# Alternating the attention scores between the two halves of the partitions and two PSUM banks, masks gathered behind them

## The chip, the cores and the metric

One core of one Trainium2 chip runs the whole program as one launch. The metric is device time in microseconds (us), the median of a few runs. The core's engines work in parallel, each through its own instruction queue in order: TensorE (PE for matmuls, PEld for weight loads), VectorE (DVE), ScalarE (ACT), GpSimd (POOL) and SyncE (SP), which issues the loads of the weights. They wait for one another on semaphores.

## The reference, cut to what matters

Two transformer blocks of two layers each run on 256 tokens of width 1024 in float32. Attention comes five times in different forms: in both layers of the first block ("sel", each query keeps its 64 best keys), then in the second block MLA and dilated attention in layer 0, differential and MoBA attention in layer 1. With one batch and 256 tokens all of them come down to this, for query tile t of 128 tokens (tile 0 sees 128 keys, tile 1 sees 256):

```
s = q @ k.T                       # per head, depth 64 (96 in MLA)
s = s + mask                      # 0 or -1e30, a key that is not allowed
p = softmax(s * scale)            # row maximum, exp, sum
out = p @ v
```

Dilated attention has 12 heads in three groups (gp) with three mask patterns; the three scores of one output head h share one softmax.

## The kernel before, in words

The weights stream through three RAW slots of 128x2048 floats. ACT rounds each to WH, DVE makes the remainder WL, and a linear layer is three matmuls for each slice (lines 1355 to 1357). All order is written out by hand: the generators put parts in one list, `order`, and each engine's program walks that list and emits its own share of every part. So the list fixes the order on every engine, and only semaphores tie the engines to each other. PSUM has eight banks; `take()` takes the first of a queue of free banks with the events that free it, `give()` puts it back at the end.

An attention is a list of units. A unit is the work of a few heads of one query tile: four heads of 128 keys or two heads of 256 keys in sel, MLA and MoBA, two heads with two maps each in differential attention, one output head with its three groups in dilated attention. `attention()` runs them as a pipeline; its step k puts these parts in the list:

1. `scores` of unit k on PE (lines 1422 to 1436) and `soft` of unit k: DVE takes the row maximum of each PSUM bank (line 1856) and scales it (line 1866), ACT takes exp for each head out of PSUM into the buffer E (line 1460, the helper for every ACT instruction).
2. `turn` of unit k-1: PE transposes the exps (line 1380), ACT or DVE copies them to PET. Ahead of them stand `pad` matmuls on the identity (line 1340), whose results nobody reads; they fill waiting time.
3. Some steps of a filler: pieces of a linear layer, gating, or the transposes of the output.
4. `values` of unit k-2: PE multiplies with v (line 1447).

T holds q and k with depth on the partitions. Heads of depth 64 lie in pairs in one row of T: an even head on partitions 0 to 63, an odd head on 64 to 127. Before the change a unit of sel and MoBA has heads of one half alone (`par`) and one bank; a dilated unit has three heads of one half in two banks; a differential unit has its first map's heads in half 0 and one bank, its second map's in half 1 and another. In every unit each head's score matmul (line 1432) is followed by its mask matmuls (line 1434: the identity in bfloat16 as weights, the mask as moving data, adding into the same bank). A dilated head of tile 1 has two masks of 128 columns. A float32 matmul shows as two records in the trace, a bfloat16 one as one.

`sel_score` (line 1401) is other work with the same operands: the index scores of the key selection, two heads of half 0 into one bank, then two of half 1 into another, first for 128 keys and then for 256, with no mask between them.

Of the kernel before, what the change touches and what calls it, by code (L numbers as in the profile page):

```python
# [29 lines left out]
B_ID, B_TRI, B_UP, B_TRI4, B_M4, B_TRI16, B_M16 = range(7)  # L30
# [13 lines left out]
def plan():  # L44
# [130 lines left out]
def program(nc, W, xd, xTd, pTd, posd, pos2d, colvd, cstd, cstbd, vecd, sgwd, smalld, out):  # L175
    with ExitStack() as ctx:
# [65 lines left out]
        def maskb(b):  # L242
            return cstb[:, b * 128:b * 128 + 128]
# [409 lines left out]
        for i in range(2):  # L653
# [36 lines left out]
            tw = []  # L690
# [33 lines left out]
            for t in range(2):  # L724
                nk = 128 * (t + 1)
                ok = {}
                ok.update(normalised(ok, MIX[:, t, 0:512].rearrange("p (h d) -> p h d", h=8), SM[t], 8, 64))
                keys_.append(ok)
                per = 4 // (t + 1)
                for par in range(2):  # L730
                    hs = [par + 2 * j for j in range(4)]
                    for a in range(0, 4, per):
                        hh = hs[a:a + per]
                        segs = [(T[64 * par:64 * par + 64, h // 2, tok(t)], T[64 * par:64 * par + 64, 4 + h // 4, 0:nk],
                                 nk, [(0, nk, selb[:, t, 0:nk])]) for h in hh]
                        outs = [(h * 64, 64, [(n_ * (t + 1) + kb, H[:, kb, 640 + (h // 4) * 64:704 + (h // 4) * 64])
                                              for kb in range(t + 1)]) for n_, h in enumerate(hh)]
                        units.append(dict(banks=[segs], joint=False, diff=False, after=tw + [("sel", (i, t))],
                                          vafter=hw[0] + hw[1], sums=[SM[t][:, h:h + 1] for h in hh], outs=outs, ok=ok,
                                          blocks=[c * 128 for c in range(per * (t + 1))]))  # L740
# [180 lines left out]
        for i in range(2):  # L921
# [9 lines left out]
            if i == 0:  # L931
# [73 lines left out]
                for t in range(2):  # L1005
# [5 lines left out]
                    for a in range(0, 8, per):  # L1011
                        hh = list(range(a, a + per))
                        segs = [(T[0:96, h, tok(t)], T[0:96, 8 + h, 0:nk], nk, [(nk - 128, 128, maskb(B_TRI))])
# [3 lines left out]
                        units.append(dict(banks=[segs], joint=False, diff=False, after=tw, vafter=mvw, ok=ok,  # L1017
# [4 lines left out]
                t_pe = [keys_[1]["op"]]  # L1022
                tw2 = []
                for t in range(2):
                    for x0, base in ((0, 0), (768, 6)):
                        tw2 += turn_T([H[:, t, x0 + h * 128:x0 + h * 128 + 128] for h in range(6)], qkr[t] + t_pe,
# [4 lines left out]
            else:  # L1031
# [46 lines left out]
                for t in range(2):  # L1078
# [4 lines left out]
                    for a in (0, 2):  # L1083
                        bks = []
                        for mp in range(2):
                            bks.append([(T[64 * mp:64 * mp + 64, h, tok(t)], T[64 * mp:64 * mp + 64, 4 + h, 0:nk], nk,
                                         [(nk - 128, 128, maskb(B_TRI))]) for h in (a, a + 1)])
# [3 lines left out]
                        units.append(dict(banks=bks, joint=False, diff=True, after=tw, vafter=dw[2][0] + dw[2][1],  # L1091
# [20 lines left out]
            for t in range(2):  # L1112
# [5 lines left out]
                if i == 0:  # L1118
                    for h in range(4):
                        segs = []  # L1120
                        for gp in range(3):
                            hd = gp * 4 + h
                            bs = 64 * (hd % 2)
                            mk = [(nk - 128, 128, maskb((B_TRI, B_TRI4, B_TRI16)[gp]))]
                            if t:
                                mk.append((0, 128, maskb((B_UP, B_M4, B_M16)[gp])))
                            segs.append((T[bs:bs + 64, hd // 2, tok(t)], T[bs:bs + 64, 6 + hd // 2, 0:nk], nk, mk))
                        outs = [(h * 64, 64, [(gp * (t + 1) + kb, H[:, kb, 1536 + (gp * 4 + h) * 64:1600 + (gp * 4 + h) * 64])
                                              for gp in range(3) for kb in range(t + 1)])]
                        units.append(dict(banks=[segs[0:2], segs[2:3]], joint=True, diff=False, after=tw2, ok=ok,  # L1130
                                          vafter=dw[2][0] + dw[2][1], sums=[SMd[t][:, h:h + 1]], outs=outs,
                                          blocks=[c * 128 for c in range(3 * (t + 1))]))
                else:
                    per = 4 // (t + 1)
                    for par in range(2):
                        hs = [par + 2 * j for j in range(4)]
                        for a in range(0, 4, per):
                            hh = hs[a:a + per]
                            segs = [(T[64 * par:64 * par + 64, 8 + h // 2, tok(t)],
                                     T[64 * par:64 * par + 64, 12 + h // 2, 0:nk], nk,  # L1140
                                     [(nk - 128, 128, maskb(B_TRI))]) for h in hh]
                            outs = [(h * 64, 64, [(n_ * (t + 1) + kb, H[:, kb, 2560 + h * 64:2624 + h * 64])
                                                  for kb in range(t + 1)]) for n_, h in enumerate(hh)]
                            units.append(dict(banks=[segs], joint=False, diff=False, after=tw2, ok=ok,
                                              vafter=dw[5][0] + dw[5][1], sums=[SMd[t][:, h:h + 1] for h in hh],
                                              outs=outs, blocks=[c * 128 for c in range(per * (t + 1))]))
# [184 lines left out]
        def tensor_program(eng):  # L1331
# [90 lines left out]
            def scores(u):  # L1422
                for k, (b, fr, cols, segs) in enumerate(u["ps"]):
# [724 lines left out]
```

## Time and profile before

| | |
|---|---|
| median of 3 runs (lowest, highest) | 1500.65 us (1500.52, 1503.26) |
| profiled execution, its own time | 1503.37 us |
| its span, from the first instruction to the last | 1501.6 us |
| PE busy | 1414.2 us, 94% |
| DVE, ACT, POOL busy | 63%, 44%, 7% |
| mean granted clock of TensorE | 0.968 of full speed |

Busy time is that in which an engine has an instruction running; the chain is the work that ended last, followed back from the end of the run through whatever released each step. In a timeline a row merges instructions of one kind: start, duration, engine, line, output and inputs, shapes as partitions x elements, count, and in brackets the idle time before it and what ended it.

### The profile page before, as it was taken

What the parts mean: (1) busy time and instruction counts of PE and PEld (TensorE: products, weight loads), DVE (VectorE), ACT (ScalarE), POOL (GpSimd) and SP (SyncE); (2) the same over time, 40 slices, a digit from 0 to 9 for tenths busy, and PEclk for the clock granted to TensorE, in tenths of its full rate; (3) what the DMA queues carried; (4) which work ended last, traced back from release to release, by engine and by line L of the source; (5) the groups of instructions that cost most, each with busy time, mean ns of one, the idle gap of its engine ahead of it and who ended that gap; (6) DMA issues with size and microseconds to landing.
All of it is one profiled execution on the core that took longest, in us unless ns stands there. A gap on an engine that the chain in (4) does not pass through costs nothing.

```text
span 1501.6 us, 16677 instructions
## 1 busy us (share of the span) xinstructions
PE 1414.2 (94%) x6765; PEld 1140.7 (76%) x6765; DVE 949.5 (63%) x1239; ACT 657.9 (44%) x886; POOL 108.9 (7%) x156
## 2 busy tenths in 40 slices
PE   6999999999998999998799898999998998899998
PEld 6767888887867888886789666788876666688886
DVE  4856777766756677765586636766665775544444
ACT  4544533333554443433455334454435434355442
POOL 1010000001020000000222200000003120000000
PEclk9989999999999999999999869999999998999999
DMA  8504688863613688872243104677763330345451
GB/s 331 189 15 188 225 294 300 296 234 128 228 41 134 228 311 293 284 272 77 102 168 113 43 0 162 247 279 261 260 219 132 120 112 1 123 161 186 177 194 56
DMA packets 40236, 269.87 MB, mean 180 GB/s; under 512 B 4544, under 2 KB 4688, under 8 KB 11872
## 3 DMA queue, kind: packets, MB, share of 16 engines
q1 hardware_dynamic: 37712, 259.31, 48.2%
q0 software_dynamic: 2304, 8.46, 1.6%
q8 instruction: 53, 0.87, 0.2%
q10 hardware_dynamic: 144, 1.05, 0.2%
q14 instruction: 23, 0.19, 0.0%
HBM read 267.75 MB, written 1.05 MB: 179 GB/s over the span
## 4 chain that ended last, share of the span: by engine, by line
PE 77%; DVE 13%; ACT 4%; issue 3%; DMA 2%; POOL 2%; SPq 0%; POOLq 0%; DVEq 0%; ACTq 0%
PE ps L1355 21%; PE ps L1357 20%; PE ps L1356 20%; PE ps L1380 4%; PE ps L1432 4%; DVE WL L1662 3%; DMA RAW<-W 2%; PE ps L1447 2%; PE ps L1340 2%; ACT WH L1460 1%; PE ps L1368 1%; PE ps L1434 1%; POOL st L1279 1%; DVE SCR L1837 1%; DVE st L1924 1%
## 5 line engine op out<-in xcount | busy, mean ns | idle before, releaser
L1662 DVE TENSOR_TENSOR WL<-RAW,WH 128x2048 fp32r<-128x2048 f32 (+5 forms) x210 | 453.3, 2161 | 279.9 <-ACT WH L1460 279.7
L1355 PE MATMUL ps<-WH,XTH 128*128 128x512 f32 (+3 forms) x1176 | 460.6, 392 | 32.7 <-DVE XTL L1667 14.0
L1460 ACT ACTIVATE WH<-RAW 128x2048 fp32r<-128x2048 f32 (+5 forms) x210 | 379.9, 1810 | 247.0 <-PE ps L1357 219.5
L1357 PE MATMUL ps<-WH,XTL 128*128 128x512 f32 (+3 forms) x1176 | 449.3, 382 | 0.0
L1356 PE MATMUL ps<-WL,XTH 128*128 128x512 f32 (+3 forms) x1176 | 448.4, 381 | 0.0
L1355 PEld LDWEIGHTS ps<-WH,XTH 128*128 128x128 f32 x1176 | 223.7, 190 | 76.3 <-DVE XTL L1667 14.2
L1357 PEld LDWEIGHTS ps<-WH,XTL 128*128 128x128 f32 x1176 | 223.4, 190 | 38.8
L1356 PEld LDWEIGHTS ps<-WL,XTH 128*128 128x128 f32 x1176 | 223.7, 190 | 37.0 <-issue 1.9
L1355 PE MATMUL ps<-WH,HTH 128*128 128x512 f32 (+1 forms) x452 | 179.6, 397 | 3.2 <-DVE HTL L1743 3.2
L1356 PE MATMUL ps<-WL,HTH 128*128 128x512 f32 (+1 forms) x452 | 178.7, 395 | 0.0
L1357 PE MATMUL ps<-WH,HTL 128*128 128x512 f32 (+1 forms) x452 | 178.6, 395 | 0.0
L1721 DVE SCALAR_TENSOR_TENSOR ACC<-RAW,colv,ACC 128x512 f32<-128x512 f32 x168 | 126.1, 751 | 5.1
L1355 PEld LDWEIGHTS ps<-WH,HTH 128*128 128x128 f32 x452 | 85.9, 190 | 22.8 <-DVE HTL L1743 3.7
L1460 ACT ACTIVATE HTH<-ps 128x512 fp32r<-128x512 f32 (+1 forms) x58 | 32.1, 586 | 160.5 <-PE ps L1380 160.3
L1357 PEld LDWEIGHTS ps<-WH,HTL 128*128 128x128 f32 x452 | 85.9, 190 | 19.7
L1356 PEld LDWEIGHTS ps<-WL,HTH 128*128 128x128 f32 x452 | 86.1, 190 | 19.2
L1277 POOL TENSOR_SCALAR st<-st 128x1 f32<-128x1 f32 (+3 forms) x42 | 21.6, 514 | 1073.0 <-DVE st L1927 547.2
L1460 ACT ACTIVATE E<-ps,st 128x128 f32<-128x128 f32 (+1 forms) x104 | 42.5, 419 | 112.0 <-DVE st L1866 112.0
L1460 ACT ACTIVATE GB<-ps 128x512 f32<-128x512 f32 (+1 forms) x94 | 46.4, 499 | 88.3 <-PE ps L1357 88.1
L1340 PE MATMUL ps<-cstb 128*128 128x512 bf16 x283 | 81.7, 412 | 0.0
L1432 PE MATMUL ps<-T 64*128 64x128 f32 (+3 forms) x208 | 71.4, 435 | 8.7 <-DVE selb L1844 4.4
L1743 DVE TENSOR_TENSOR HTL<-ps,HTH 128x512 fp32r<-128x512 f32 x54 | 35.8, 687 | 37.7 <-ACT HTH L1460 37.7
(175 smaller groups left out, 1124.0 us busy)
## 6 DMA issues: line engine op xcount, KB each, us to landing
RAW<-W SPq DMA_DIRECT2D x220, 1024.0 KB, 4.8
RAW<-W SPq DMA_DIRECT2D x7, 960.0 KB, 4.7
RAW<-W SPq DMA_DIRECT2D x6, 910.0 KB, 5.8
RAW<-W SPq DMA_DIRECT2D x9, 576.0 KB, 3.5
VEC<-vecd POOLq DMA_DIRECT2D x10, 512.0 KB, 6.1
RAW<-W SPq DMA_DIRECT2D x8, 512.0 KB, 3.3
RAW<-W SPq DMA_DIRECT2D x6, 546.0 KB, 4.3
GB<-xTd ACTq DMA_DIRECT2D x1, 1024.0 KB, 8.4
```

The lines of the kernel that those rows point to most:

```text
L1277: eng.tensor_scalar(x, x, scale, eps, ALU.mult, ALU.add).then_inc(*own.up())
L1340: eng.matmul(banks[b][:, :], identb, cstb[:, 0:512], start=True, stop=True)
L1355: eng.matmul(ps, xh, hi[:, j, c0:c0 + cw], start=first and j == 0, stop=False)
L1356: eng.matmul(ps, xh, lo[:, j, c0:c0 + cw], start=False, stop=False)
L1357: op = eng.matmul(ps, xl, hi[:, j, c0:c0 + cw], start=False, stop=last and j == n - 1)
L1380: op = eng.transpose(banks[b][0:rows, j * 128:j * 128 + 128], src, ident)
L1432: op = eng.matmul(banks[b][:, c:c + nk], q, ks, start=True, stop=True)
L1447: op = eng.matmul(banks[b][:, c0:c0 + dv], PET[:, u["i"], blk * 128:blk * 128 + 128], val, start=(j == 0), stop=(j == len(lst) - 1))
L1460: return eng.activation(dst, src, f, **k)
L1662: eng.tensor_tensor(WL[:, p, 0:w], RAW[:, n % NRAW, 0:w], WH[:, p, 0:w].bitcast(F32), ALU.subtract).then_inc(*up("wl", n))
L1721: op = eng.scalar_tensor_tensor(out=ACC[:, a, :], in0=view[:, j, :], scalar=cond[:, kt:kt + 1], in1=ACC[:, a, :], op0=ALU.mult, op1=ALU.add)
L1743: eng.tensor_tensor(HTL[:, r2:r2 + 2, :], banks[b][:, :].rearrange("p (n q) -> p n q", n=2), HTH[:, r2:r2 + 2, :].bitcast(F32), ALU.subtra ...
```

## The change

Heads are grouped so that a unit has heads of both halves of the partitions. A unit of sel and MoBA now holds the same number of heads as before, half of them from each half, in two banks instead of one. Dilated heads are stored in another order (`PAIRED`; the columns of the weights are reordered on the host, in chunks of the same width), so that an output head's groups 0 and 1 lie in the two halves of one row of T, and group 2 in half h % 2. `scores` now waits for all banks of the unit first, then issues one score per bank in turn, and puts the masks behind all scores: one mask matmul for each bank where the heads share a mask (`same`, broadcast over the heads), one for each head in dilated attention, where the two masks of tile 1 become one of 256 columns. MLA keeps one bank and its order of scores.

```diff
+PAIRED = [g * 4 + h for h in range(4) for g in range(2)] + [8 + h for h in range(4)]
-B_ID, B_TRI, B_UP, B_TRI4, B_M4, B_TRI16, B_M16 = range(7)
+B_ID, B_UP, B_TRI, B_M4, B_TRI4, B_M16, B_TRI16 = range(7)
...
-            all_rows("even_w_in_2", 0, 1024, (2208, 2592), (2592, 2976), (672, 1056))
-            all_rows("even_w_in_2", 0, 1024, (1056, 1440), (1440, 1824), (1824, 2208))
+            q1, q2, k1, k2 = ([(x0 + c * 64, x0 + c * 64 + 64) for c in PAIRED[n:n + 6]] for x0 in (672, 1440)
+                              for n in (0, 6))
+            all_rows("even_w_in_2", 0, 1024, (2208, 2592), (2592, 2976), q1, q2, k1, k2)
...
-                per = 4 // (t + 1)
-                for par in range(2):
-                    hs = [par + 2 * j for j in range(4)]
-                    for a in range(0, 4, per):
-                        hh = hs[a:a + per]
...
+                per = 2 // (t + 1)
+                for a in range(0, 4, per):
+                    hh = [par + 2 * j for par in range(2) for j in range(a, a + per)]
+                    segs = [(T[64 * (h % 2):64 * (h % 2) + 64, h // 2, tok(t)],
+                             T[64 * (h % 2):64 * (h % 2) + 64, 4 + h // 4, 0:nk], nk, (0, nk, selb[:, t, 0:nk]))
+                            for h in hh]
...
+                    units.append(dict(banks=[segs[0:per], segs[per:]], joint=False, diff=False, same=True,
...
+                        order3 = (0, 1, 2) if h % 2 else (0, 2, 1)
...
+                            bs, row = (64 * (h % 2), 4 + h // 2) if gp == 2 else (64 * gp, h)
+                            mk = ((0, 256, maskb((B_UP, B_M4, B_M16)[gp], 2)) if t else
+                                  (0, 128, maskb((B_TRI, B_TRI4, B_TRI16)[gp])))
...
+                        at_ = 1 if h % 2 else 2
+                        units.append(dict(banks=[segs[0:at_], segs[at_:]], joint=True, diff=False, same=False, after=tw2,
...
-                    for (c, nk, _), (q, ks, _, masks) in zip(cols, segs):
-                        op = eng.matmul(banks[b][:, c:c + nk], q, ks, start=True, stop=True)
-                        for c0, w, mk in masks:
-                            op = eng.matmul(banks[b][:, c + c0:c + c0 + w], identb, mk, start=False, stop=True,
+
+                for n in range(max(len(segs) for _, _, _, segs in u["ps"])):
+                    for b, _, cols, segs in u["ps"]:
+                        if n < len(segs):
+                            (c, nk, _), (q, ks, _, _) = cols[n], segs[n]
+                            eng.matmul(banks[b][:, c:c + nk], q, ks, start=n == 0, stop=True, skip_group_check=True)
+                for k, (b, _, cols, segs) in enumerate(u["ps"]):
+                    n, nk = len(segs), segs[0][2]
+                    view = banks[b][:, 0:n * nk].rearrange("p (n k) -> p n k", n=n)
+                    if u["same"]:
+                        c0, w, mk = segs[0][3]
+                        op = eng.matmul(view[:, :, c0:c0 + w], identb, mk.unsqueeze(1).broadcast_to([128, n, w]),
+                                        start=False, stop=True, skip_group_check=True)
+                    else:
+                        for j in range(n):
+                            c0, w, mk = segs[j][3]
+                            op = eng.matmul(view[:, j, c0:c0 + w], identb, mk, start=False, stop=True,
                                             skip_group_check=True)
                     op.then_inc(*up("score", (u["id"], k)))
```

MoBA's units are regrouped in the same way as those of sel.

## Rows read from the trace of the kernel before

**Rows 1.** The page: PE busy, and the chain that ended last by engine.

```profile
PE 1414.2 (94%) x6765; PEld 1140.7 (76%) x6765; DVE 949.5 (63%) x1239; ACT 657.9 (44%) x886; POOL 108.9 (7%) x156
...
PE 77%; DVE 13%; ACT 4%; issue 3%; DMA 2%; POOL 2%; SPq 0%; POOLq 0%; DVEq 0%; ACTq 0%
```

**Rows 2.** Busy time in stretches: length, PE, PEld, DVE, ACT, POOL; PEclk is granted clock.

```profile
74.30:84.30 10.00, 10.00 (x34) 5.96 (x34) 4.69 (x6) 6.28 (x21) 5.84 (x6) 0.50 0.00 0
84.50:108.00 23.50, 23.50 (x145) 18.05 (x144) 12.12 (x24) 8.33 (x22) 0.00 (x0) 1.00 0.07 22
...
852.50:889.90 37.40, 37.40 (x128) 24.04 (x129) 10.90 (x39) 10.97 (x47) 0.00 (x0) 0.50 0.00 0
...
1251.90:1261.90 10.00, 10.00 (x34) 6.07 (x34) 3.63 (x9) 4.52 (x21) 0.00 (x0) 0.50 0.00 1
```

**Rows 3.** Timeline of PE: one sel unit of two heads of 256 keys, then pads.

```profile
85.00 0.70 PE L1432 MATMUL ps<-T 64*128 64x256 f32 x2
...
85.84 0.70 PE L1432 MATMUL ps<-T 64*128 64x256 f32 x2
...
86.59 0.59 PE L1340 MATMUL ps<-cstb 128*128 128x512 bf16 x2
```

**Rows 4.** Chain in order of time: one float32 matmul of 512 columns, start and duration.

```profile
786.12 0.86 PE ps L1420 x2
```

**Rows 5.** Timeline of PE: the eight index scores, and the matmul behind them.

```profile
51.23 1.65 PE L1401 MATMUL ps<-T 64*128 64x128 f32 x16 [0.56 <-DVE T L1735]
52.81 0.50 PE L1355 MATMUL ps<-WH,XTH 128*128 128x512 f32 x1
```

**Rows 6.** Weight loads of line 1432: least, median and greatest ns.

```profile
L1432 PEld LDWEIGHTS ps<-T x208: 182/186/335, 72.8 to 1270.9; 64*128 64x128 f32 x88, 96*128 96x128 f32 x16
```

**Rows 7.** Timeline, dilated units: tile 0, tile 1, and the last of tile 1.

```profile
862.13 0.79 PE L1432 MATMUL ps<-T 64*128 64x128 f32 x2
...
864.83 1.06 PE L1340 MATMUL ps<-cstb 128*128 128x512 bf16 x2
...
874.73 1.22 PE L1432 MATMUL ps<-T 64*128 64x256 f32 x2
...
879.02 1.06 PE L1340 MATMUL ps<-cstb 128*128 128x512 bf16 x2
...
891.46 0.70 PE L1432 MATMUL ps<-T 64*128 64x256 f32 x2
...
893.90 0.59 PE L1340 MATMUL ps<-cstb 128*128 128x512 bf16 x2
```

**Rows 8.** Timeline of PE, differential units: scores of a tile-0 unit, pads, the tail.

```profile
1204.04 0.49 PE L1432 MATMUL ps<-T 64*128 64x128 f32 x2
...
1206.26 0.59 PE L1340 MATMUL ps<-cstb 128*128 128x512 bf16 x2
...
1241.69 1.12 PE L1380 MATMUL ps<-cst,E 128*128 128x128 f32 x4 [5.18 <-DVE E L1885]
```

**Rows 9.** Timeline, first units of three attentions: their last exp, then their transposes.

```profile
80.10 0.37 ACT L1460 ACTIVATE E<-ps,st 128x128 f32<-128x128 f32 x1
...
82.78 1.06 PE L1380 MATMUL ps<-cst,E 128*128 128x128 f32 x4
...
426.27 0.37 ACT L1460 ACTIVATE E<-ps,st 128x128 f32<-128x128 f32 x1
...
427.56 1.06 PE L1380 MATMUL ps<-cst,E 128*128 128x128 f32 x4
...
1254.54 0.37 ACT L1460 ACTIVATE E<-ps,st 128x128 f32<-128x128 f32 x1
...
1255.95 1.06 PE L1380 MATMUL ps<-cst,E 128*128 128x128 f32 x4
```

**Rows 10.** Row maxima by shape: busy us and mean ns of one.

```profile
L1856 DVE TENSOR_REDUCE st<-ps 128x2 f32<-128x512 f32 x24 | 16.5, 690 | 23.6 <-PE ps L1434 23.5
...
L1856 DVE TENSOR_REDUCE st<-ps 128x2 f32<-128x256 f32 x8 | 3.4, 423 | 9.9 <-PE ps L1434 9.9
```

More of the change, by code:

```diff
@@ L728, in program @@
                 keys_.append(ok)
-                per = 4 // (t + 1)
-                for par in range(2):
-                    hs = [par + 2 * j for j in range(4)]
-                    for a in range(0, 4, per):
-                        hh = hs[a:a + per]
[L734 to L740, printed above, removed]
+                per = 2 // (t + 1)
[4 more added lines that the diff above has]
+                            for h in hh]
+                    outs = [(h * 64, 64, [(n_ * (t + 1) + kb, H[:, kb, 640 + (h // 4) * 64:704 + (h // 4) * 64])
+                                          for kb in range(t + 1)]) for n_, h in enumerate(hh)]
+                    units.append(dict(banks=[segs[0:per], segs[per:]], joint=False, diff=False, same=True,
+                                      after=tw + [("sel", (i, t))], vafter=hw[0] + hw[1],
+                                      sums=[SM[t][:, h:h + 1] for h in hh], outs=outs, ok=ok,
+                                      blocks=[c * 128 for c in range(2 * per * (t + 1))]))
             def gating():
@@ L1016, in program @@
                                               for kb in range(t + 1)]) for n_, h in enumerate(hh)]
-                        units.append(dict(banks=[segs], joint=False, diff=False, after=tw, vafter=mvw, ok=ok,
+                        units.append(dict(banks=[segs], joint=False, diff=False, same=True, after=tw, vafter=mvw, ok=ok,
                                           sums=[SMm[t][:, h:h + 1] for h in hh], outs=outs,
@@ L1025, in program @@
                     for x0, base in ((0, 0), (768, 6)):
-                        tw2 += turn_T([H[:, t, x0 + h * 128:x0 + h * 128 + 128] for h in range(6)], qkr[t] + t_pe,
+                        tw2 += turn_T([H[:, t, x0 + n * 128:x0 + n * 128 + 128] for n in range(6)], qkr[t] + t_pe,
                                       base, t, pad=0 if t or base else 13)
@@ L1086, in program @@
                             bks.append([(T[64 * mp:64 * mp + 64, h, tok(t)], T[64 * mp:64 * mp + 64, 4 + h, 0:nk], nk,
-                                         [(nk - 128, 128, maskb(B_TRI))]) for h in (a, a + 1)])
+                                         (nk - 128, 128, maskb(B_TRI))) for h in (a, a + 1)])
                         s4 = col(4)
@@ L1090, in program @@
                                                 for kb in range(t + 1)]) for n_, h in enumerate((a, a + 1))]
-                        units.append(dict(banks=bks, joint=False, diff=True, after=tw, vafter=dw[2][0] + dw[2][1],
+                        units.append(dict(banks=bks, joint=False, diff=True, same=True, after=tw, vafter=dw[2][0] + dw[2][1],
                                           s4=s4, nk=nk, sums=[s4[:, j:j + 1] for j in range(4)], outs=outs, ok=ok,
@@ L1119, in program @@
                     for h in range(4):
+                        order3 = (0, 1, 2) if h % 2 else (0, 2, 1)
                         segs = []
[L1121 to L1131, printed above, removed]
+                        for gp in order3:
+                            bs, row = (64 * (h % 2), 4 + h // 2) if gp == 2 else (64 * gp, h)
+                            mk = ((0, 256, maskb((B_UP, B_M4, B_M16)[gp], 2)) if t else
+                                  (0, 128, maskb((B_TRI, B_TRI4, B_TRI16)[gp])))
+                            segs.append((T[bs:bs + 64, row, tok(t)], T[bs:bs + 64, 6 + row, 0:nk], nk, mk))
@@ new lines, in program @@
+                        outs = [(h * 64, 64, [(n_ * (t + 1) + kb, H[:, kb, 1536 + (gp * 4 + h) * 64:1600 + (gp * 4 + h) * 64])
+                                              for n_, gp in enumerate(order3) for kb in range(t + 1)])]
+                        at_ = 1 if h % 2 else 2
+                        units.append(dict(banks=[segs[0:at_], segs[at_:]], joint=True, diff=False, same=False, after=tw2,
+                                          ok=ok, vafter=dw[2][0] + dw[2][1], sums=[SMd[t][:, h:h + 1]], outs=outs,
@@ L1132, in program @@
                                           blocks=[c * 128 for c in range(3 * (t + 1))]))
                 else:
[L1134 to L1146, printed above, removed]
+                    per = 2 // (t + 1)
@@ new lines, in program @@
+                    for a in range(0, 4, per):
+                        hh = [par + 2 * j for par in range(2) for j in range(a, a + per)]
+                        segs = [(T[64 * (h % 2):64 * (h % 2) + 64, 8 + h // 2, tok(t)],
+                                 T[64 * (h % 2):64 * (h % 2) + 64, 12 + h // 2, 0:nk], nk,
+                                 (nk - 128, 128, maskb(B_TRI))) for h in hh]
+                        outs = [(h * 64, 64, [(n_ * (t + 1) + kb, H[:, kb, 2560 + h * 64:2624 + h * 64])
+                                              for kb in range(t + 1)]) for n_, h in enumerate(hh)]
+                        units.append(dict(banks=[segs[0:per], segs[per:]], joint=False, diff=False, same=True, after=tw2,
+                                          ok=ok, vafter=dw[5][0] + dw[5][1], sums=[SMd[t][:, h:h + 1] for h in hh],
+                                          outs=outs, blocks=[c * 128 for c in range(2 * per * (t + 1))]))
```

6 lines of the change are left out of this document (3 added, 3 removed).

## The prediction

> **What bounds the kernel now.** I read the page first: PE is busy for 94% of the span and holds 77% of the chain that ended last [rows 1]. The reader is to see that time taken from PE is likely to come off the end, but only where PE does not wait. So the table of stretches comes next: during the sel units of tile 1 and during the dilated attention PE is busy without a gap, at the full clock in the one and at half of it in the other [rows 2]. Last come the timelines of the five attentions, for what one unit costs and what ends each wait [rows 3, 7 to 9].
>
> **What a score and a mask cost.** A float32 matmul of 512 columns takes 0.86 us in its two records [rows 4], so streaming costs 0.84 ns a column and record: a head of 256 keys streams 2 x 0.214 us, one of 128 keys 2 x 0.107. A mask is one bfloat16 record at half that, 0.107 for 256 columns, 0.053 for 128 (an estimate from the same row). A sel head of tile 1 takes 85.84 - 85.00 = 0.84 us [rows 3] where streaming is 0.43 + 0.11 = 0.54. So 0.30 us of each head is exposed: the first load, and draining before and after the mask. Four 128-key heads take 2.21 us [rows 8], 0.55 each, of which 0.27 streams: again some 0.28. At half clock a dilated head takes (879.02 - 874.73)/3 = 1.43 in tile 1 and 2.70/3 = 0.90 in tile 0 [rows 7]; twice the streaming is 1.07 and 0.53, so 0.37 is exposed.
>
> **Do the two halves run at once?** The units do not show it, since a mask that needs all rows stands behind each score. The index scores do: eight heads, half 0 and half 1, two banks, no mask. They take 52.81 - 51.23 = 1.58 us [rows 5]; streamed one after the other they would need 4 x 0.214 + 4 x 0.43 = 2.57. With the halves side by side it is 1.29 + 0.30 exposed once = 1.59. The ends for the new order are therefore full overlap and none. I take full overlap: the row fits to 0.01 us, and there the halves even come in groups, not in turn. For heads in the same half it also says that a load costs nothing beyond streaming. The Trainium skill says otherwise ("TensorE: Matmul & The Clock Gate", Part 3, on what overlaps): a weight load runs beside matmuls in flight only where the row group differs. By that rule each half of the index scores would pay 7 loads of 0.186 [rows 6] on top of 1.29, some 2.6 us; the trace shows 1.58, so the sum goes without it. It is a rival below.
>
> **The change part by part.** A unit afterwards costs its exposed time once, the longer half's stream, and the masks' stream.
>
> - *sel and MoBA, tile 1* (two heads of 256, one per half): 0.30 + 0.43 + 0.21 = 0.94, some 0.05 for the second half's later start: 1.0 instead of 1.59 [rows 3]. Saved 0.6 a unit. PE is never idle there [rows 2] and the exp of a unit is needed only a unit later, after pads, transposes, values and the next scores. Eight sel units: 4.8.
> - *sel and MoBA, tile 0* (four heads): 0.30 + 0.43 + 0.21 = 0.94 instead of 2.21. But these two units open the attention, and their softmax waits for DVE and ACT work of another kind ahead of it in the queues. Unit 0's last exp ends at 80.47, 426.64 and 1254.91 and its transposes run at 82.78, 427.56 and 1255.95 [rows 9]. So scores, now off the path, can give back at most that slack: 2.3, 0.9 and 1.0, less about 0.2 for a second row maximum (2 x 0.423 - 0.690 [rows 10]) and the read of the last sum: 2.0, 0.6 and 0.8. PE then idles some 2 to 4 us where scores and pads stood.
> - *Differential, tile 0*: 2.21 to 0.94, 1.27 twice; tile 1, by the head of [rows 3] with its mask of 128 columns about 3.1 to 0.30 + 0.86 + 0.21 = 1.4, 1.7 each. Behind the last unit PE waits 5.18 us for DVE [rows 8]: that saving only lengthens the wait. 4.2.
> - *Dilated*: tile 0 at half clock 2.70 to 0.37 + 0.85 + 0.32 = 1.54, tile 1 4.29 to 0.37 + 1.71 + 0.64 = 2.72; at full clock 2.44 [rows 7] to 0.30 + 0.86 + 0.32 = 1.48. The first two units open a stage and wait for their exps: 1.5 for both. Then 2 x 1.16 + 3 x 1.57 + 0.96 = 8.0. Together 9.5.
> - *MoBA*: 0.8 + 1.2 for the unit at half clock + 3 x 0.6 = 3.8.
> - *MLA* has ten mask matmuls fewer, no new overlap. Bounds 0 and 10 x 0.30; its rows of 96 partitions and the DVE work behind it put it near the lower: 0.5.
> - *Waits*: `scores` waits for both banks before its first matmul, and all of PE stands behind it. Six banks circulate in sel and MoBA, and a step takes three instead of two; so a unit takes banks freed a step earlier. Only where the output's transposes take two more does its second bank come from the exps just before, and 2.5 us of PE work lie between. The row maximum of a first bank starts only behind all masks; that is hidden by the same work, and if the cover were gone would cost 0.4 to 0.7 a unit. Both at nothing.
> - *Nothing* for the reordered columns (as many loads of the same size, no queue order changed), the mask table, the flags, the unchanged exps, transposes and values.
>
> At the clocks of before that is 2.0 + 0.6 + 4.8 + 4.2 + 9.5 + 3.8 + 0.5 = 25.4 us.
>
> **The clock.** Dilated attention runs at 0.50, the 1.2 GHz level, from 852.5 to 889.9 with PE never idle [rows 2]: 64-row scores with drains between them fill half of it. The sel stage of tile 1, scores a smaller part, stays at 1.00. By 891.46 a unit runs at full-clock times again [rows 7]. Afterwards the 4.29 us of scores in a unit become 2.72, with both halves working and one drain in place of three. The stage would be some 29 us at half clock (37.4 less what the units inside it save) and, by 2.44 against 4.29 for the same scores [rows 7], some 16 at full. So the clock gives 0 to 13; I take 8, that it returns in the first third. Against that the new idling at the openings may hold half clock a little longer in sel and MoBA (74.3 to 84.3 and 1251.9 to 1261.9 now [rows 2]): 0 to 3, I take 1, as pads and dense scores follow at once.
>
> Sum: 25.4 + 8 - 1 = 32.4. The profiled execution took 1503.4 (span 1501.6 and 1.8 around it): 1471. The median shown is 2.7 lower, and by it the same sum gives 1468. I say 1470.
>
> **The rivals.**
>
> 1. *The dilated stage stays at half clock.* For it: PE was gapless there and yet slow. Against: what filled it is what the change takes away. 1503.4 - 24.4 = 1479.
> 2. *The halves do not overlap when they alternate*, only the drains go. Then a unit saves one exposed time fewer than its heads: 0.3 a pair, 0.9 for four, 0.7 for three. 8 x 0.3 + 2.6 + 2.7 (differential) + 6 (dilated) + 1.8 (MoBA) + 0.5 = 16, or 1487 with the clock as now. Against: [rows 5].
> 3. *Loads in the same half are exposed* (mechanism: two heads of one half in a bank, three later records each, 0.186 a load [rows 6], at 3 differential, 6 dilated units that count): 9 x 0.56 = 5 less, 1476. This is the case that the skill's page above would make.
> 4. *The clock falls at the openings and stays down*, as it did in dilated attention: PE idles 2 to 4 us in three openings, and two of those openings already show 0.50 [rows 2]. If the rest of both sel stages (23.5 us now, 21 each after the savings) ran at 1.2 GHz, it would cost up to 42 us: 1503.4 - 32 + 42 = 1513. It decides from three quarters of the two stretches on. Against: the same stage came back to 1.00 at 84.5 before [rows 2], with less dense scores.
>
> **How the numbers follow.** Forecast 0.52, rival 1 0.27, rival 2 0.10, rival 3 0.05, rival 4 0.06 (in full or in part). No change to be told is within 0.2%, 3 us. Faster by more: 0.94; same 0.03; slower 0.03. The forecast's own range is 1461 (all of the clock's 13, no losses) to 1477; 8 in 10 reach from 1460 to 1482, which takes in rivals 1 and 3 and leaves out most of 2 and all of 4.
>
> **What the profile afterwards would show.** Records of two scores of one unit start within 0.1 us of each other, and a sel unit of tile 1 takes about 1.0 us up to its pads, a dilated one 1.5 or 2.7. The transposes of the first sel unit follow its last exp at once. The wait before the last differential transposes is longer than 5.18. The dilated stage shows a granted clock above 0.50 on average. I am wrong if a unit's scores still take the sum of their streams, if the wait for exps shows up in front of every transpose, or if PEclk is lower than before in the sel or MoBA stages.

## The result, and the profile after

The changed kernel takes 1465.79 us (median of four runs, 1465.35 to 1466.13) against 1501.95 for the kernel before beside it (1500.52 to 1506.81): a ratio of 0.9764, 95% interval 0.9732 to 0.9797. The profiled executions are 1465.74 and 1503.37, so 37.6 us are to be found in the two traces; the forecast was 1470, by a sum of 32.4. Single executions of the kernel before differ by their granted clock: of 54 made beside the experiments, eight at a mean clock of 0.977 took 1488 to 1491 us and seven at 0.963 or 0.964 took 1507 to 1510, while eight of the changed kernel stand at 0.978 to 0.981 and 1465 to 1468.

The page after, PE's busy time and the chain by engine; PE has lost 50 us of busy time, and five points of the chain [rows 1]:

```profile
PE 1364.7 (93%) x6723; PEld 1111.9 (76%) x6723; DVE 948.0 (65%) x1257; ACT 657.1 (45%) x886; POOL 108.7 (7%) x156
...
PE 72%; DVE 14%; ACT 6%; issue 3%; DMA 2%; POOL 2%; SPq 0%; DVEq 0%; ACTq 0%; POOLq 0%
```

Stretches of the trace after (columns as in [rows 2]): the opening of the first sel attention, its units of tile 1, the whole dilated attention, the opening of MoBA.

```profile
72.80:79.60 6.80, 6.33 (x28) 3.35 (x28) 3.48 (x8) 4.39 (x8) 6.28 (x10) 0.50 0.10 37
82.90:106.00 23.10, 22.73 (x157) 18.21 (x156) 13.03 (x30) 8.90 (x24) 0.00 (x0) 1.00 0.08 24
844.60:866.40 21.80, 20.20 (x150) 15.12 (x151) 10.25 (x40) 11.46 (x49) 0.00 (x0) 1.00 0.00 1
1219.60:1226.40 6.80, 5.38 (x23) 3.94 (x24) 2.26 (x7) 4.26 (x21) 0.00 (x0) 0.50 0.00 1
```

The third row is the largest change: 37.4 us of this stage stood at 0.50 [rows 2], and now none of it does; in the trace of the second run of the changed kernel (after_again, below) 21.8 us of it stand at 1.00 as well. The two openings still stand at 0.50.

PE's timeline after, in the order of the trace: first sel transposes of layer 0; a sel unit of tile 1; first sel transposes of layer 1; the first dilated unit, then one of tile 0, one of tile 1 and the last one; a differential unit of tile 0 and the tail of the last; MoBA's first transposes.

```profile
81.05 0.66 PE L1383 MATMUL ps<-cst,E 128*128 128x128 f32 x4 [1.11 <-ACT E L1476]
...
86.50 0.70 PE L1439 MATMUL ps<-T 64*128 64x256 f32 x4
87.14 0.39 PE L1445 MATMUL ps<-selb,cstb 128*128 128x256 bf16 x2
87.37 0.59 PE L1343 MATMUL ps<-cstb 128*128 128x512 bf16 x2
...
422.55 1.11 PE L1383 MATMUL ps<-cst,E 128*128 128x128 f32 x4 [4.03 <-ACT E L1476]
...
844.63 0.68 PE L1439 MATMUL ps<-T 64*128 64x128 f32 x6 [0.56 <-ACT T L1476]
...
851.29 0.71 PE L1439 MATMUL ps<-T 64*128 64x128 f32 x6
...
852.11 0.59 PE L1343 MATMUL ps<-cstb 128*128 128x512 bf16 x2
...
856.71 1.13 PE L1439 MATMUL ps<-T 64*128 64x256 f32 x6
...
858.12 0.59 PE L1343 MATMUL ps<-cstb 128*128 128x512 bf16 x2
...
866.40 0.59 PE L1343 MATMUL ps<-cstb 128*128 128x512 bf16 x2
...
1173.45 0.59 PE L1343 MATMUL ps<-cstb 128*128 128x512 bf16 x2
...
1207.60 1.11 PE L1383 MATMUL ps<-cst,E 128*128 128x128 f32 x4 [7.44 <-DVE E L1901]
...
1221.02 1.12 PE L1383 MATMUL ps<-cst,E 128*128 128x128 f32 x4 [3.38 <-ACT E L1476]
```

A unit is now one group of scores, then one group of masks, then the pads. From first score to pads a sel unit of tile 1 takes 87.37 - 86.50 = 0.87 us, where it was 1.59 [rows 3]; a dilated unit 0.82 in tile 0 and 1.41 in tile 1, where these were 2.70 and 4.29 at half clock and 2.44 for one of tile 1 at full clock [rows 7]. Where the same work has a row in both traces, the difference of its starts says what has been saved up to there:

| place | before | after | saved so far |
|---|---|---|---|
| first sel transposes, layer 0 [rows 9] | 82.78 | 81.05 | 1.7 |
| first sel transposes, layer 1 [rows 9] | 427.56 | 422.55 | 5.0 |
| fourth dilated unit [rows 7] | 862.13 | 851.29 | 10.8 |
| pads behind the last dilated unit [rows 7] | 893.90 | 866.40 | 27.5 |
| pads behind the second differential unit [rows 8] | 1206.26 | 1173.45 | 32.8 |
| last differential transposes [rows 8] | 1241.69 | 1207.60 | 34.1 |
| first MoBA transposes [rows 9] | 1255.95 | 1221.02 | 34.9 |
| end of the profiled execution | 1503.4 | 1465.7 | 37.6 |

PE's waits after, by line and releaser: in all, times, longest. The first was not there before; the second was 5.18 [rows 8].

```profile
PE ps L1383 <- ACT E L1476: 9.8, 5, 4.0
...
PE ps L1383 <- DVE E L1901: 7.4, 1, 7.4
```

### The profile page after: what moved, and what is told of

It reads as the page before. It is cut to its first block, busy times and chain, and to the rows that moved or that the text cites. A ratio compares the mean times of both kernels' runs of the same rounds, so it can differ in the third digit from the quotient of the medians.

```text
span 1463.9 us, 16616 instructions
## 1 busy us (share of the span) xinstructions
PE 1364.7 (93%) x6723; PEld 1111.9 (76%) x6723; DVE 948.0 (65%) x1257; ACT 657.1 (45%) x886; POOL 108.7 (7%) x156
## 4 chain that ended last, share of the span: by engine, by line
PE 72%; DVE 14%; ACT 6%; issue 3%; DMA 2%; POOL 2%; SPq 0%; DVEq 0%; ACTq 0%; POOLq 0%
PE ps L1358 21%; PE ps L1360 21%; PE ps L1359 21%; PE ps L1383 4%; DVE WL L1678 3%; DMA RAW<-W 2%; ACT WH L1476 2%; ACT E L1476 1%; PE ps L1371 1%; PE ps L1463 1%; POOL st L1282 1%; PE ps L1439 1%; DVE st L1872 1%; PE ps L1343 1%; ACT XTH L1476 1%
## 5 line engine op out<-in xcount | busy, mean ns | idle before, releaser
L1343 PE MATMUL ps<-cstb 128*128 128x512 bf16 x283 | 78.1, 398 | 0.0
L1282 POOL TENSOR_TENSOR st<-st,cst 128x1 f32<-128x1 f32 (+3 forms) x42 | 47.2, 1124 | 3.5
```

Of the source, the lines that this page charges most:

```text
L1282: eng.tensor_tensor(x, x, MH.to_broadcast([128, x.shape[1]]), ALU.pow).then_inc(*up("rsqrt", key))
L1343: eng.matmul(banks[b][:, :], identb, cstb[:, 0:512], start=True, stop=True)
```

## The experiments

My account was that a run of scores pays its exposed time once, that the two halves stream side by side, and that this density brings the clock back in the dilated stage. The rivals: drains alone, order alone, or a clock that came back for another reason. Four kernels take the change apart. The experiments ran on four chips, each beside the kernel before; so times of two experiments are compared directly only in a rough way, or through their ratios.

**gather_alone**: the units of before, masks behind all scores of a bank.

```
-for (c, nk, _), (q, ks, _, masks) in zip(cols, segs):
-    op = eng.matmul(banks[b][:, c:c + nk], q, ks, start=True, stop=True)
+for n, ((c, nk, _), (q, ks, _, _)) in enumerate(zip(cols, segs)):
+    eng.matmul(banks[b][:, c:c + nk], q, ks, start=n == 0, ...)
+for (c, nk, _), (_, _, _, masks) in zip(cols, segs):
     for c0, w, mk in masks:
```

> The kernel before with its own units and order of heads (one half of the partitions for each unit, but for differential and MLA), its masks alone gathered behind the scores of each bank. Theory of the forecast (what a unit pays is its exposed time once for a run of scores without masks between, and the halves side by side are a gain of their own): a sel unit of tile 1 takes 0.30 + 0.86 + 0.21 = 1.4 us instead of 1.6 (now 0.86), and the whole is 1487 us with the dilated stage at half clock as before; if fewer drains are enough to bring the clock back, 1474 to 1479. Rival A (the drains alone are the gain, the alternating order adds nothing): 1466, with a sel unit at 0.9. Rival B (drains cost nothing, only the halves count): 1500 or more.

Measured: 1491.17 us (ratio 0.9939, 0.9902 to 0.9975). Two units of its timeline (sel tile 1; a dilated one at full clock), and its dilated stage:

```profile
89.67 1.13 PE L1432 MATMUL ps<-T 64*128 64x256 f32 x4
...
90.96 0.59 PE L1340 MATMUL ps<-cstb 128*128 128x512 bf16 x2
...
878.02 1.13 PE L1432 MATMUL ps<-T 64*128 64x256 f32 x4
...
880.16 0.59 PE L1340 MATMUL ps<-cstb 128*128 128x512 bf16 x2
```

```profile
853.50:886.00 32.50, 32.48 (x166) 22.93 (x167) 12.99 (x44) 11.73 (x49) 0.00 (x0) 0.74 0.00 1
```

A sel unit takes 1.29: one exposed time of 0.30 gone, two streams in a row left. So gathering is worth 0.30 of the 0.72 a unit, the halves the other 0.42. The clock of the stage is 0.74, between the two kernels: in this execution its units run at full clock from 874.09 on, in the kernel before only from 890.08. The whole is 4 us above the 1487 that I gave for a stage at half clock. In this trace nothing is left, at the first dilated score, of what the sel units saved (853.51, against 850.64 before); the first sel unit of tile 1, for one, runs at half clock here, 83.24 to 85.65, and ran at full before. I have not traced the loss further.

**mask_each**: the changed order and banks, each mask behind its own score.

```
 for n in range(...):
     for k, (b, _, cols, segs) in enumerate(u["ps"]):
         if n < len(segs):
             eng.matmul(banks[b][:, c:c + nk], q, ks, start=n == 0, ...)
+            op = eng.matmul(banks[b][:, c + c0:c + c0 + w], identb, mk, ...)
```

> The changed kernel with its units, banks and alternating order, but each head's mask right behind its score, as before. Theory of the forecast: a mask takes all rows, so it keeps the next half's score from running beside this one; no overlap and no drain saved, a sel unit of tile 1 back at 1.5 to 1.6 us, the dilated stage back at half clock, 1495 to 1503 us (dilated tile 1 has three mask records instead of six). Rival A (overlap of the halves needs only alternating order): a sel unit near 1.1, 1475 to 1485. Openings wait as before, not as after.

Measured: 1499.67 us (ratio 0.9992, 0.9956 to 1.0029). Timeline: a sel unit, an MLA unit of the same size, and its dilated stage:

```profile
89.15 0.70 PE L1439 MATMUL ps<-T 64*128 64x256 f32 x2
...
89.99 0.70 PE L1439 MATMUL ps<-T 64*128 64x256 f32 x2
...
90.73 0.59 PE L1343 MATMUL ps<-cstb 128*128 128x512 bf16 x2
...
815.92 0.60 PE L1439 MATMUL ps<-T 96*128 96x256 f32 x2
...
816.95 0.59 PE L1343 MATMUL ps<-cstb 128*128 128x512 bf16 x2
```

```profile
855.50:899.00 43.50, 43.47 (x151) 27.97 (x152) 12.30 (x43) 11.73 (x49) 0.00 (x0) 0.57 0.00 0
```

The second score starts 0.84 us behind the first, as before [rows 3], though it is of the other half: alternating alone is worth nothing. The two parts of the change are not two gains that add; without the gathering the halves cannot meet.

**halves_grouped**: as changed, the scores bank by bank instead of in turn.

```
-for n in range(max(len(segs) for _, _, _, segs in u["ps"])):
-    for b, _, cols, segs in u["ps"]:
-        if n < len(segs):
+for b, _, cols, segs in u["ps"]:
+    for n in range(len(segs)):
```

> The changed kernel, but the scores of a unit go bank by bank (all of one half, then all of the other) instead of in turn; masks stay behind all. It differs only in units with two heads in a bank. Theory of the forecast (the index scores of the kernel before overlap fully in groups): within 1 us of the changed kernel, 1465 to 1467, and four-head units at 0.8 to 0.9 us. Rival (only neighbours in the queue overlap, so one score more streams alone: 0.21 us in four-head units of 128 keys, 0.43 in those of 256): 1467 to 1469, four-head units at 1.05, differential ones of tile 1 at 1.7.

Measured: 1468.54 us (1466.49 to 1469.11; ratio 0.9786, 0.9740 to 0.9831), against 1467.09 (1465.73 to 1468.39) of the control below. Its second differential unit, eight records of four heads, and the pads behind it:

```profile
1173.46 0.72 PE L1438 MATMUL ps<-T 64*128 64x128 f32 x8
1174.11 0.39 PE L1444 MATMUL ps<-cstb 128*128 128x256 bf16 x2
1174.34 0.59 PE L1343 MATMUL ps<-cstb 128*128 128x512 bf16 x2
```

0.88 us, as in the changed kernel (1173.45 - 1172.58 = 0.87). The third unit, four heads of 256 keys, takes 1.31 (1185.99 to 1187.30), where the rival said 1.7 and the changed kernel takes 1.30 (1185.10 to 1186.40). What counts is that both halves stand in one run of scores with no mask between; that they alternate does not. No run puts heads of both halves into one bank, so whether the two banks are needed is not shown.

**dilated_mask_each**: as changed, but in the dilated attention alone with each mask behind its score (the loop of mask_each where the unit is a joint one).

> The changed kernel, but in the dilated attention alone each mask stands right behind its score again; all else as changed. Theory of the forecast, after the result (the dilated stage gained some 21 us, of which its records explain 9 to 10 and the clock the rest): the stage goes back to half clock and the whole to 1483 to 1487 us. Rival (the clock there returned for another reason, such as the shorter opening or the new order of the columns, so only the records are lost): 0.7 to 1.0 us for each of six units that count, 1471 to 1473, with the stage at full clock.

Measured: 1486.23 us (1483.77 to 1489.20; ratio 0.9910, 0.9879 to 0.9942). One of its units and its stage:

```profile
873.09 1.22 PE L1440 MATMUL ps<-T 64*128 64x256 f32 x2
...
877.37 1.06 PE L1343 MATMUL ps<-cstb 128*128 128x512 bf16 x2
```

```profile
849.70:889.00 39.30, 39.29 (x154) 25.38 (x155) 12.60 (x44) 11.73 (x49) 0.00 (x0) 0.65 0.00 0
```

A unit is back at 4.28 us and the stage at half clock for most of its length. By the medians 19 to 20 us, half of the whole gain, hang on the masks of eight units. The traces show 17 of them in the stage itself, which takes 38.7 us from its first score (849.71) to the pads of its last unit (888.38) instead of 21.8; another 5 lie ahead of it in this execution, in code that is the same in both kernels.

**dense_before**: nothing of the change; the kernel before with eight idle matmuls instead of two in each dilated unit.

```
-attention(units, 0.125, fill, first=3 if i else 0)
+attention(units, 0.125, fill, first=3 if i else 0, pads=() if i else (8,) * 8)
```

> The kernel before with nothing of the change, but eight idle matmuls (bfloat16, 512 columns, 0.215 us each at full clock) instead of two ahead of the transposes of each dilated unit: work added, to see what the clock alone is worth. Theory (in the dilated stage of before the clock stands at half because its scores of 64 rows with masks between fill too little of PE, and that costs as much as the records do): the stage runs at full clock, a masked unit of tile 1 takes 2.4 instead of 4.3 us; some 17 us come back and 6 x 0.215 x 8 = 10 go out, so 1494 to 1499 us, below the kernel before although work was added. Rival (the clock there has another cause): the stage stays at half clock, the pads cost 0.43 each, 1518 to 1524.

Measured: 1500.90 us (ratio 1.0009, 0.9978 to 1.0040). The stage's first score, a unit, the pads of the last unit (cut off at 892), and the stage:

```profile
853.81 0.46 PE L1432 MATMUL ps<-T 64*128 64x128 f32 x2 [0.76 <-DVE T L1735]
...
871.18 0.70 PE L1432 MATMUL ps<-T 64*128 64x256 f32 x2
...
873.62 1.89 PE L1340 MATMUL ps<-cstb 128*128 128x512 bf16 x8
...
891.41 0.81 PE L1340 MATMUL ps<-cstb 128*128 128x512 bf16 x3
```

```profile
853.80:892.00 38.20, 37.81 (x198) 23.25 (x203) 13.65 (x45) 12.15 (x49) 0.00 (x0) 0.91 0.00 1
```

The whole missed my range by 2 us and is not below the kernel before. The mechanism shows in the rows: an unchanged unit falls from 4.29 to 2.44, and from its first score (853.81) to the pads of its last unit (891.41) the stage takes 37.6 us with 7 x 6 x 0.215 = 9 us of added pads, where before it took 850.64 to 893.90, 43.3. So in these two executions the stage is 5.7 us shorter with work added; 3.2 of them were lost ahead of it, in code that is the same. The clock alone is worth some 43.3 - (37.6 - 9) = 15 us. The estimate is too high by what pads in the openings' waits did not cost, and too low because the stage still stands at 0.91 and not at 1.00. At an equal mean clock the pads show their price: three executions of this kernel at 0.976 took 1500 to 1503 us, two of the kernel before at 0.976 took 1491.

**no_pads**: as changed, without the two idle matmuls of a unit (default 2 to 0).

> The changed kernel without the two idle matmuls ahead of the transposes of a unit, in the sel, MLA, dilated and MoBA attentions (30 units; those given by hand, eight in the first sel unit and the differential ones, stay). Theory (scores are now dense enough to hold the clock by themselves): about 26 units on the path x 0.43 = 11 us less, 1453 to 1457. Rival (the pads are what holds the clock in the dilated stage, where scores are only a quarter of the time): that stage falls to half clock again and gives back 12 to 17 us, 1465 to 1472.

Measured: 1466.76 us (1465.86 to 1467.52; ratio 0.9772, 0.9728 to 0.9816). Its dilated stage and its MoBA units:

```profile
841.00:867.00 26.00, 22.73 (x145) 17.97 (x145) 11.69 (x44) 11.73 (x49) 0.00 (x0) 0.80 0.00 1
1212.90:1234.00 21.10, 17.19 (x98) 13.33 (x99) 9.77 (x26) 8.41 (x33) 1.21 (x2) 0.68 0.00 1
```

The time lies in the rival's range, its mechanism came only in part. The clock of the dilated stage is 0.80 instead of 1.00, not 0.50, and that of MoBA 0.68 instead of 0.83 (its row stands under filled_waits). The dilated stage gives back 2.9 us and not 12 to 17: its first score comes 3.6 us earlier than in the changed kernel, the projection behind it 0.7 (866.99, against 867.68). The same time comes out with less work done: there the pads earn what they cost.

**late_split**: as changed, with the step that rounds the second operand (ACT, then 1.60 us on DVE) behind the first two sel units.

```
-do("p_split", i, list(pt_free))      # ahead of attention(...)
+do("p_split", i, list(pt_free))      # in gating(), behind its two halves
```

> The changed kernel with one step moved: the rounding and the remainder of the projection's second operand (ACT PTH, then DVE PTL, 1.60 us) stand behind the first two units of sel attention in the queues instead of in front of their row maxima. Theory (the new wait of PE for exps in front of the first sel transposes comes from DVE, which reads the first scores only after that remainder): 1.5 to 2 us less in each of two layers, 1462 us, and the wait of 4.0 us at layer 1 falls to about 2. Rival (the table load and the layer norm ahead of the exps on ACT end it, not DVE): nothing, 1465 to 1466.

Measured: 1471.01 us (1469.70 to 1471.06; ratio 0.9797, 0.9760 to 0.9834). All four executions lie above all four of the control, on the same chip; the intervals of the ratios overlap.

```profile
78.43 0.66 PE L1383 MATMUL ps<-cst,E 128*128 128x128 f32 x4 [0.51 <-ACT E L1476]
80.91 2.05 PE L1414 MATMUL ps<-GB,T 128*128 128x128 f32 x8 [1.82 <-POOL GB L1314]
```

The first transposes come 2.6 us earlier (81.05 to 78.43), so DVE was what held the exps up. But gating, next in PE's queue, then waits 1.82 for the layer norm on POOL; at 2.05 us its eight matmuls run at half clock (1.16 in the changed kernel), and the next sel unit, 82.89 to 84.45, takes 1.56 instead of 0.87. The output projection of this layer starts at 97.85, 3.3 us later than in the changed kernel.

**early_mask**, on the reading that gating waited for its mask on DVE, sets that mask ahead and keeps late_split's edit.

> The changed kernel with two DVE steps changing places around the sel attention: the masking of the gating weights (1.21 us) goes in front, where DVE waits 3.3 us for ACT, and the remainder of the second operand (1.60 us) behind the first two units. As in the run that moved only the latter, the first sel transposes come 2 to 2.6 us earlier; the difference is that gating no longer stands behind a DVE step. Theory (that run was slower because PE then idled between transposes and gating and so kept half clock over the next units): PE goes on without a gap, 1462 to 1464 us. Rival (the clock stays low at the openings whatever stands there): 1469 to 1471, as that run.

Measured: 1469.98 us (1468.79 to 1471.00; ratio 0.9786, 0.9732 to 0.9839).

```profile
79.14 0.66 PE L1383 MATMUL ps<-cst,E 128*128 128x128 f32 x4 [0.98 <-ACT E L1476]
80.57 1.13 PE L1414 MATMUL ps<-GB,T 128*128 128x128 f32 x8 [0.78 <-POOL GB L1314]
```

That reading was wrong: POOL still ends the wait. The units behind keep full clock here, yet at the end of the attention nothing is left of the 1.9 us: the first matmul of the output projection starts at 94.56, and at 94.53 in the changed kernel. Why the whole is 3 us slower than the control, which ran on another chip, and than the two kernels that follow, which ran on the same one, is left open.

**few_pads** (no pads in the last four sel units of a layer and in MLA) and **early_few** (with early_mask's edit):

> The changed kernel without idle matmuls ahead of the transposes in the last four sel units of each layer and in MLA; they stay in the first two sel units, in the dilated and in the MoBA attention. Theory (after the run without any: where the clock is high and scores dense the pads are pure loss, in the dilated and the MoBA stage they pay for themselves by the clock): what the run without pads had gained up to the dilated stage, 2 to 3.5 us, is kept: 1462 to 1464. Rival (it is lost again further on because the stages behind wait for something else): 1465 to 1467.

> Both of the edits above in one kernel. If they add: 1459 to 1462 us. If the pads taken out are what the clock needs behind the earlier transposes: 1466 to 1472.

Measured: 1467.01 us both (1464.86 to 1467.84 and 1465.12 to 1468.41; ratios 0.9764 and 0.9762). Neither can be told from the control: few_pads came out where its rival said, early_few in the range given for edits that do not add. At the end of either sel attention of few_pads the output projection waits 0.85 us for DVE, and in MLA the last transposes wait 2.42 for ACT: much of what the pads took had been such waits.

**after_again**, the control:

> The changed kernel itself, as the control of the others on this chip: 1465 to 1467 us.

Measured: 1467.09 us (1465.73 to 1468.39; ratio 0.9773, 0.9735 to 0.9810).

**filled_waits**: as changed, with more idle matmuls where PE waits anyway.

```
-attention(..., pads=(8,), first=8 if i else 3)
+attention(..., pads=(22 if i else 11,), first=8 if i else 3)
-pads=(2, 2, 12, 6))
+pads=(2, 2, 12, 30))
-attention(units, 0.125, fill, first=3 if i else 0)
+attention(units, 0.125, fill, first=3 if i else 0, pads=(14,) if i else ())
```

> The changed kernel with more idle matmuls where PE waits anyway: ahead of the first transposes of the sel attention (11 and 22 instead of 8), of MoBA (14 instead of 2) and of the last differential unit (30 instead of 6), each count chosen to fit into the wait that the profile shows there at full clock (1.1, 4.0, 3.4 and 7.4 us). Theory (what the openings still lose is the half clock behind their waits): the units behind run at full clock, some 1 us in sel 0, 2 in sel 1, 2 to 2.5 behind differential and in MoBA, 1458 to 1462 us. Rival (PE is given the next wait instead, or the clock falls a little later): 1465 to 1468.

Measured: 1462.83 us (six runs, 1461.43 to 1466.35; ratio 0.9753, 0.9715 to 0.9791). Granted clock 0.986 to 0.991. The opening of sel in layer 1 and MoBA, first in this kernel, then in the changed one:

```profile
412.00:430.00 18.00, 15.04 (x96) 9.13 (x96) 12.51 (x34) 11.89 (x35) 7.77 (x12) 1.00 0.17 61
1215.00:1235.00 20.00, 19.81 (x129) 13.74 (x129) 10.26 (x27) 10.44 (x38) 1.21 (x2) 0.91 0.00 1
```

```profile
412.00:430.00 18.00, 12.31 (x74) 8.22 (x71) 10.71 (x33) 11.30 (x35) 7.75 (x12) 0.81 0.10 30
1215.00:1235.00 20.00, 16.30 (x108) 11.86 (x109) 9.82 (x26) 8.39 (x33) 1.21 (x2) 0.83 0.00 1
```

Here the clock holds, or comes back earlier: by the two traces 2.2 us are gained between the output projections of layers 0 and 1, and 1.9 more up to the projection behind MoBA. In sel of layer 0 the edit failed:

```profile
81.11 0.66 PE L1383 MATMUL ps<-cst,E 128*128 128x128 f32 x4 [3.40 <-ACT E L1476]
...
83.56 1.23 PE L1439 MATMUL ps<-T 64*128 64x256 f32 x4
```

The wait of 1.1 us that was to be filled belongs to an opening at half clock. In this execution the opening ran at full clock, so its 11 idle matmuls ended 3.4 us too early, the next unit ran at half clock and the output projection of the layer starts 1.6 us later (96.17, against 94.53). The median of the whole is 3 to 4 us below the two of the changed kernel, and five of its six runs lie below all eight of that kernel; but the control ran on another chip and the intervals of the ratios overlap, so by these the two cannot be told apart.

## Why the prediction held, point by point

Two rows of the kernel before that the points below rest on: its first dilated score, and a stretch behind its first differential unit.

```profile
850.64 0.46 PE L1432 MATMUL ps<-T 64*128 64x128 f32 x2 [0.79 <-DVE T L1735]
```

```profile
1197.20:1200.60 3.40, 3.40 (x10) 2.62 (x9) 1.69 (x8) 2.90 (x9) 0.00 (x0) 0.50 0.00 0
```

- *Full overlap of the halves, and no price for loads in the same half* (rivals 2 and 3). Right. A unit of two halves takes 0.87 where the sum said 1.0, one of four heads 0.87 where it said 0.94, a dilated one at full clock 1.41 where it said 1.48. Rival 2 was in effect built as gather_alone: it came to 1491, where the rival said 1487, with the clock partly back.
- *The openings, 2.0, 0.6 and 0.8.* Right in kind: the scores came off the path only until the exps were late, which is the new wait of 9.8 us on ACT. Measured 1.7 at layer 0 and 0.8 at MoBA by the table.
- *sel and its followers.* From the first transposes of layer 0 to those of layer 1 the sum said 2.4 + 0.6 = 3.0; 3.3 came. From there to the first dilated score it said 2.4 + 0.5 for MLA, and 1.0 came: behind the new wait of 4.03 us the next sel unit of layer 1 runs at half clock, 425.36 to 426.93, 1.57 us, where before it ran at full, and so do the gating matmuls in front of it (1.98 instead of 1.42); these are 1.3 of the 1.9 that are missing.
- *Dilated, 9.5, and the clock, +8.* From the first score (850.64 before, 844.63 after) to the last unit's pads the stage went from 43.26 to 21.77: 21.5 instead of 17.5. The mechanism was right and rival 1 wrong; the clock term was too small. With the 9.5 kept, the clock gave 12, near its upper bound of 13: it did not return in the first third, it never fell. Of the 4.0 that the sum lacks 2.2 lie ahead of the fourth unit: 4.8 were saved there, where the sum had 1.5 + 1.16, because I took the first two units to be bound by exps.
- *Differential, 4.2.* For the first two units the sum had 1.27 each; 1.37 and 1.35 came. But the table shows 5.3 from the end of the dilated stage to there. 1.6 more lie between the two units, where linear layers of before run at half clock from 1197.2 to 1200.6. The eight matmuls that follow the first unit, from 1196.81 on, take 4.4 us at a mean clock of 0.61 in the traces of before, mask_each and dense_before, the three kernels that keep a mask behind each differential score, and 2.8 at 1.00 in those of all others; so this goes with the change, and the sum did not have it. The last 1.0 lies ahead of the first differential score (1194.65 before, 1166.15 after), where linear layers run at a mean clock of 0.98 before and 0.99 after. Spells of half clock there come and go from trace to trace where the code is the same: one stretch of linear layers behind a wait for DVE has 1.00 in the changed kernel (901.5 to 906.1) and 0.59 in dilated_mask_each (923.9 to 928.5). So I count this 1.0 as luck. The last unit's saving did only lengthen the wait for DVE, 5.18 to 7.44.
- *MoBA, 3.8.* 0.8 at the opening and 2.7 behind it.
- *Half clock at the openings, -1, and rival 4.* The openings do stand at 0.50, for 6.8 us in sel of layer 0 and in MoBA, but the stages come back, as the sum had it. Over the whole attention the mean clock goes from 0.81 to 0.85 in sel of layer 0, from 0.86 to 0.85 in layer 1 and from 0.78 to 0.82 in MoBA; the loss of 1 that the sum had for this came in sel of layer 1 (1.3, above).
- *Waits of the bank queue, at nothing.* PE's waits in front of scores (L1439, 7.8 us in all) name the selected mask and the transposed operands, no reader of a bank.

So the sum lacks 5.2 us of the 37.6, and the 1470 that I said lies 4.3 above the profiled execution. The clock term of the dilated stage is 4.0 of the 5.2; the stretch behind the first differential unit gave 1.6 and the linear layers ahead of it 1.0 that were not in the sum; sel of layer 1 with MLA fell short by 1.9, about half of which is the loss that the sum had put down as 1. The other differences are small and of both signs. The lower end of my range was a slip: 25.4 + 13 taken from the median is 1462 and not 1461. Before's best-clocked runs (0.977) lie 21 to 25 us above the changed kernel's medians, which is near the 25.4 that the sum had at the clocks of before; no trace of such a run exists, so what its stages did is not shown.

## What to carry to other kernels

Group matmuls of 64 rows by what they need of the array: all scores of both halves in one run (here with a bank for each half), then all that need every row; the order within the run made no difference here. Before costing a PE change, look at the granted clock of its stage: here a third of the gain or more was clock, work could be taken out (no_pads) or put in (dense_before) without moving the time, and in late_split a shorter path to the first softmax made the whole slower. Idle matmuls where the engine waits anyway held the clock behind two openings; the 3 to 4 us that this seems to be worth are not told apart from the control.

## What the runs showed of the hardware

The exposed 0.30 us is not a price of every mask. In mask_each two heads of 256 keys with 64 rows take 1.58 us, and two with 96 rows, masks between them too (of 128 columns instead of 256, some 0.1 less to stream), take 816.95 - 815.92 = 1.03. So the exposed time goes with the change between scores on half of the rows and masks on all. The Trainium skill ("TensorEngine Tiling (Array Packing)", Tiling Modes, Key Properties) says that changing the tiling mode, and not only the tile, drains the engine; these rows agree, with some 0.4 us for two heads.

In halves_grouped scores of the second half stand in the queue behind all those of the first, and the group takes no longer than in turn, 0.88 against 0.87 us with 128 keys and 1.31 against 1.30 with 256. The index scores of before, which come in groups too, had suggested it [rows 5]; so two scores need not be neighbours in the queue to overlap.
